# Seven-product down projection in five up steps instead of seven or eight, its weights loaded earlier, and four half products moved behind the last up product

## The reference

```python
def conv_ffn(x, w_up, conv_k, conv_b, w_down):        # first block, D_FF = 2816
    h = x @ w_up                                      # 1024 -> 2 * 2816
    ...
    h = sum(hp[:, j:j + S] * conv_k[j] for j in range(CONV_W)) + conv_b
    a, b = jnp.split(h, 2, axis=-1)
    return (jax.nn.gelu(a, approximate=False) * b) @ w_down

def swiglu(xn, w_gate, w_up, w_down):                 # second block, D_FF_2 = 2816
    return (jax.nn.silu(xn @ w_gate) * (xn @ w_up)) @ w_down
```

## Time and profile before

| what | value |
|---|---|
| median of 3 runs | 3492.47 us (3491.96 to 3493.58) |
| profiled execution: its time, its span | 3492.06 us, 3490.3 us |
| TensorE busy | 3372.2 us, 97% of the span, 16655 matmuls and transposes |
| VectorE, ScalarE busy | 2205.2 us (63%), 1475.6 us (42%) |
| mean granted TensorE clock | 0.991 of full speed |
| mean HBM traffic | 90 GB/s |

### The profile page before, as it was taken

The page is one execution under the profiler, slowest core; times in us unless marked ns, Lnnn a source line. Parts: engine busy times, 40 slices in busy tenths (PEclk is TensorE's granted clock), DMA queues, the critical chain, the costliest instruction groups (busy, mean ns, idle before and its releaser), DMA issues. The chain is left out here.

```text
span 3490.3 us, 42076 instructions
## 1 busy us (share of the span) xinstructions
PE 3372.2 (97%) x16655; PEld 2815.0 (81%) x16655; DVE 2205.2 (63%) x3566; ACT 1475.6 (42%) x2577; POOL 252.3 (7%) x319
## 2 busy tenths in 40 slices
PE   9999999999999999999999999999999999999999
PEld 7888888877788888888777777888888887888887
DVE  5644566777766545677777686554666697545665
ACT  4543333433335433334333564544343574543332
POOL 1300210000023002000000020100000000100000
PEclk9999999999999999999999999999999999999999
DMA  4112342232131122413221222423222212413321
GB/s 159 58 52 72 104 159 66 103 103 97 61 122 61 52 79 95 162 61 109 97 97 61 84 70 79 130 63 119 86 85 102 96 43 66 130 55 106 105 103 61
DMA packets 84148, 315.14 MB, mean 90 GB/s; under 512 B 10096, under 2 KB 10864, under 8 KB 78832
## 3 DMA queue, kind: packets, MB, share of 16 engines
q1 hardware_dynamic: 83952, 312.46, 27.2%
HBM read 308.23 MB, written 4.19 MB: 90 GB/s over the span
## 5 line engine op out<-in xcount | busy, mean ns | idle before, releaser
L1344 PE MATMUL bk<-xh,wh 128*128 128x512 f32 (+1 forms) x2216 | 838.3, 378 | 5.7 <-DVE xl L2070 5.6
L1344 PE MATMUL bk<-xh,wl 128*128 128x512 f32 (+1 forms) x2216 | 830.3, 375 | 0.0
L1344 PE MATMUL bk<-xl,wh 128*128 128x512 f32 (+1 forms) x2216 | 830.0, 375 | 0.0
L2057 DVE TENSOR_TENSOR wl<-wr,wh 128x1024 fp32r<-128x1024 f32 (+1 forms) x300 | 361.9, 1215 | 302.4 <-ACT wh L1650 301.1
L1344 PEld LDWEIGHTS bk<-xh,wh 128*128 128x128 f32 x2216 | 418.0, 189 | 79.8 <-issue 4.1
L1344 PEld LDWEIGHTS bk<-xh,wl 128*128 128x128 f32 x2216 | 417.6, 188 | 75.6
L1344 PEld LDWEIGHTS bk<-xl,wh 128*128 128x128 f32 x2216 | 418.0, 189 | 72.1
L1650 ACT ACTIVATE wh<-wr 128x1024 fp32r<-128x1024 f32 (+1 forms) x300 | 310.2, 1043 | 313.8 <-PE bk L1344 218.7
L2063 DVE SCALAR_TENSOR_TENSOR wl<-wr,par,wh 128x512 fp32r<-128x512 f32 (+1 forms) x360 | 249.3, 737 | 166.5 <-ACT wh L1656 165.3
L1623 ACT ACTIVATE wh<-ar 128x1024 fp32r<-128x1024 f32 (+1 forms) x168 | 141.1, 843 | 487.0 <-DVE ar L2028 271.0
L1656 ACT ACTIVATE wh<-wr,par 128x512 fp32r<-128x512 f32 (+1 forms) x360 | 236.1, 708 | 202.4 <-PE bk L1344 153.4
(11 more groups left out here) (292 smaller groups left out, 5368.1 us busy)
## 6 DMA issues: line engine op xcount, KB each, us to landing
wr<-in_wpk SPq DMA_DIRECT2D x468, 512.0 KB, 3.6
ar<-in_wdn SPq DMA_DIRECT2D x36, 1024.0 KB, 7.8
gb<-in_ln_g SPq DMA_DIRECT2D x6, 512.0 KB, 4.5
gb<-in_ln_b SPq DMA_DIRECT2D x6, 512.0 KB, 6.3
ar<-in_xT SPq DMA_DIRECT2D x8, 256.0 KB, 7.3
wr<-in_wpk SPq DMA_DIRECT2D x8, 256.0 KB, 6.2
ar<-in_memT SPq DMA_DIRECT2D x2, 1024.0 KB, 4.7
x<-in_x SPq DMA_DIRECT2D x4, 512.0 KB, 5.2
```

The lines of the kernel that those rows point to most:

```text
L1344: i = pe.e.matmul(dst, lw, rw, start=g not in opened, stop=end)
L2057: dve.e.tensor_tensor(m.wl[:, s, a], m.wr[:, r, a], m.wh[:, s, a].bitcast(F32), ALU.subtract) \
```

## The change

Three things are changed in every one of the four FFNs.

1. In phases 0 and 1 the fourteen half products followed the up steps in numbers 0, 2, 2, 2 (first pair) and 2, 2, 2, 2 (second pair), none in the third pair. Now they follow in 0, 3, 3, 3 and 3, 2, 0, 0: five up steps of the eight. The next phase's three raw down transfers stood in up steps 1, 2 and 3 of the third pair; now they stand in up steps 2 and 3 of the second pair and 0 of the third.
2. In phase 2 the numbers were 0, 3, 3, 2 for pair 9 and 3, 3, 0, 0 for pair 10. Now they are 0, 3, 3, 2 and 2, 0, 0, 0, and the last four half products (7a, 7b, 4a, 4b) stand behind pair 10's last up step.
3. So that pairs 9 and 10 can be split before products 7 and 4 have read the old hidden values, their split values go to places that these two products don't read: three quarters where the sums were, one quarter behind the buffer. `hid_hi` and `hid_lo` of these pairs become two instructions each (768 and 256 columns), and wait for product 3 instead of 4. Pair 9's are put in up steps 1 and 2 of pair 10, pair 10's behind 7a and 7b.

```diff
-        def made(pair, seven=None, per=(0, 0, 0, 0), after=0, loads=None):
+        def made(pair, seven=None, per=(0, 0, 0, 0), loads={}):
             for step, _ in enumerate(ups(2 * pair)):
-                if loads is not None and step in (1, 2, 3):
-                    self.add("down_load", *loads, 3 * loads[0].ph + step - 1, l)
+                if step in loads:
+                    self.add("down_load", *loads[step], l)
                 if seven is None:
                     if self.soon:
                         self.add(*self.soon.pop(0))
-                elif step < 2 and pair % 3 == 0 and self.soon:
+                elif self.soon and (pair % 3 == 0 and step < 2 or pair == 10 and step > 0):
                     self.add(*self.soon.pop(0))
...
         made(0)
-        made(1, loads=(F[0], None))
+        made(1, loads={n + 1: (F[0], None, n) for n in range(3)})
         made(2)
-        for ph in range(3):
-            products = self.seven(F[ph])
-            pair = 3 * ph + 3
-            made(pair, products, (0, 2, 2, 2) if ph < 2 else (0, 3, 3, 2))
-            if ph < 2:
-                made(pair + 1, products, (2, 2, 2, 2))
-                drive((products, 1))
-                made(pair + 2, loads=(F[ph + 1], F[ph]))
-            else:
-                held, self.soon = self.soon, []
-                steps = ups(2 * pair + 2)
-                for step in range(4):
-                    next(steps)
-                    if step < 2:
-                        for _ in range(3):
-                            next(products, None)
-                    if step == 1:
-                        drive((products, 1))
-                        self.soon = held
-                    elif self.soon:
-                        self.add(*self.soon.pop(0))
-                drive((steps, 1))
-                self.soon += [("hid_hi", si, 10), ("hid_lo", si, 10)]
+        for ph in range(2):
+            products, pair = self.seven(F[ph]), 3 * ph + 3
+            made(pair, products, (0, 3, 3, 3))
+            made(pair + 1, products, (3, 2, 0, 0), {n + 2: (F[ph + 1], F[ph], pair + n) for n in range(2)})
+            made(pair + 2, loads={0: (F[ph + 1], F[ph], pair + 2)})
+        products = self.seven(F[2])
+        made(9, products, (0, 3, 3, 2))
+        made(10, products, (2, 0, 0, 0))
+        for _ in products:
+            if self.soon:
+                self.add(*self.soon.pop(0))
...
     def hid(self, side, pair, b, n):
-        a = pair % 3 * 1792 + b * 256
+        a = pair % 3 * 1792 + b * 256 if b < 7 else 5376 + (pair - 9) * 256
...
     def hid_hi(si, pair):
         if pair >= 3:
-            act.wait_ge(*ev["grp7", si, pair // 3 - 1, 4, 1])
+            act.wait_ge(*ev["grp7", si, pair // 3 - 1, 4 if pair < 9 else 3, 1])
```

More of the change, by code:

```diff
@@ L1316, in mm @@
                         pe.wait_ge(*ev["hid", G.si, kb // 2])
-                        xh, xl = (m.hid(side, kb // 2, 2 * (kb % 2), 512).unsqueeze(1) for side in (m.hh, m.hl))
-                        kb = 0
+                        b, at = 2 * (kb % 2) + o // 2, o % 2 * 128
+                        xh, xl = (m.hid(side, kb // 2, 4 + b, 256)[:, at:at + 128] for side in (m.hh, m.hl))
                     elif G.op == "branch" and G.base == 8:
@@ L1338, in mm @@
                 else:
-                    seq = [(xh[:, kb, tile(o)], wh[:, kk, :]), (xh[:, kb, tile(o)], wl[:, kk, :]),
-                           (xl[:, kb, tile(o)], wh[:, kk, :])]
+                    if G.op != "hid":
+                        xh, xl = xh[:, kb, tile(o)], xl[:, kb, tile(o)]
+                    seq = [(xh, wh[:, kk, :]), (xh, wl[:, kk, :]), (xl, wh[:, kk, :])]
                     dst = ps[:, 0:cols]
@@ L1631, in hid_hi @@
                 act.wait_ge(*ev["prod", si, 2 * pair + p])
-            act.e.activation(m.hid(m.hh, pair, 0, 1024), m.z(si, pair), ACT.Copy) \
+            z = m.z(si, pair)
+            act.e.activation(m.hid(m.hh, pair, 4, 768), z[:, 0:768], ACT.Copy)
+            act.e.activation(m.hid(m.hh, pair, 7, 256), z[:, 768:1024], ACT.Copy) \
                 .then_inc(*ev.up("x_hi", ("hid_hi", si, pair)))
@@ L2011, in hid_lo @@
         dve.wait_ge(*ev["hid_hi", si, pair])
-        i = dve.e.tensor_tensor(m.hid(m.hl, pair, 0, 1024), m.z(si, pair), m.hid(m.hh, pair, 0, 1024).bitcast(F32),
+        if pair >= 9:
+            z = m.z(si, pair)
+            dve.e.tensor_tensor(m.hid(m.hl, pair, 4, 768), z[:, 0:768], m.hid(m.hh, pair, 4, 768).bitcast(F32),
                                 ALU.subtract)
-        if pair >= 9:
-            i.then_inc(*ev.up("x_lo", ("hid", si, pair)))
+            dve.e.tensor_tensor(m.hid(m.hl, pair, 7, 256), z[:, 768:1024], m.hid(m.hh, pair, 7, 256).bitcast(F32),
+                                ALU.subtract).then_inc(*ev.up("x_lo", ("hid", si, pair)))
             return
+        dve.e.tensor_tensor(m.hid(m.hl, pair, 0, 1024), m.z(si, pair), m.hid(m.hh, pair, 0, 1024).bitcast(F32),
+                            ALU.subtract)
         dve.e.tensor_tensor(m.hid(m.hl, pair, 4, 768), m.zx[pair % 2], m.hid(m.hh, pair, 4, 768).bitcast(F32),
```

## The result

The changed kernel takes 3460.59 us (median of 4 runs, 3458.5 to 3461.48) against 3492.58 us before: a ratio of 0.9907, interval 0.989 to 0.9924. It is 32.0 us faster. I had forecast 3451 with a range of 3441 to 3466; the likeliest case's own range, 3446 to 3457, does not hold it. The profiled execution took 3458.5 us, 33.6 less than the profiled one of before and 2.1 less than the median of its own kernel.

The account below looks back on a forecast made before the run. TensorE, busy for 97% of the span, was taken as the bound, so only its gaps and half-clock time could pay. -36.0 + 16.2 - 21.2 = -41.0 us gave 3451 us, range 3441 to 3466 (8 in 10).

Parts of the forecast that it names:

- the likeliest case: The prediction's own case, all three parts as summed: 3451 us, own range 3446 to 3457, chance 0.67.
- The late starts: Phases 1 and 2 of the first two FFNs: earlier down transfers make four starts prompt, giving back 36.0 us.
- The gaps between 2b and 5a: Phases 0 and 1: 5a waits for product 2's additions, adding 2.02 us in each of eight phases, +16.2 us.
- the rival's 13 us: Rival at the eight new gaps: half clock follows each, 1.67 us apiece, 13.4 us in all, 3464.5 us; chance 0.10.
- A wrong bound in that step: Lower bound of each new gap between 2b and 5a: one addition (0.73 us) and the refill, about 1 us.
- The FFN end: End of all four FFNs: waits for the split of pairs 9 and 10 and excess time go, -21.2 us.
- The chain I built: First FFN's end: ScalarE and VectorE work up to pair 10's weight split, done E + 13.4, due 13.6 us.
- E: The end time of the last up step at the FFN end, from which the prediction counts pair 10's preparation.
- the rivals: Five outcomes: clock falls (0.10), pair 10's split late (0.08), shorter gaps (0.07), starts still late (0.05), transfers starve up steps (0.03).

Follow-up runs that it names:

- e1: The kernel before with only the three down transfers moved to where the change has them: 3460.07 us, ratio 0.9909.
- e3: The changed kernel with the three down transfers back in up steps 1, 2 and 3 of the third pair: 3484.61 us, ratio 0.9977.
- e11: The changed kernel with product 4's two additions moved behind the first token tile's residual additions and norm: 3459.48 us, ratio 0.9903.
- e6: The changed kernel with product 2's two additions put ahead of the weight split on VectorE: 3440.36 us, ratio 0.9847.
- e4: The kernel before with only the FFN end changed (last four half products, places of pairs 9 and 10): 3473.82 us, ratio 0.9947.
- e7: The changed kernel with half products of phases 0 and 1 at 0, 4, 2, 3 and 3, 2, 0, 0: 3440.46 us, ratio 0.9847.

## Why the prediction was right, and where its sizes were off

- **The late starts.** Right in mechanism and nearly in size. The transfer held the evacuation: e1 gave 32.4 us, the sum said 36.0, and 2.8 of the difference are the gaps that grew in phase 2. The wait that I had worked out as 0.2 us is 0.16 us in the trace, but a wait costs more than its length: from one matmul start to the next, each start keeps 0.42 us, 0.9 us more in all.
- **The gaps between 2b and 5a.** Right in place and number (eight new ones), too small in size: 16.2 forecast, 19.8 us in the trace. The unit of 2.02 us was taken, for the first two FFNs, from phases that had just started late, and a late start gave VectorE time to catch up. With prompt starts the gap is 2.51 us in phases 1 and 2 of the first two FFNs, the old phase 2 included (e1 shows the same lengthening, with its spread untouched), and with late ones it is 2.02 again (e3, with the dense spread). In phase 1 ScalarE's high split ahead of the gap now waits for VectorE's differences, where in phase 0 it waited for TensorE:

```profile
769.57 1.06 ACT L1612 ACTIVATE wh<-ar 128x1024 fp32r<-128x1024 f32 x1 [2.58 <-DVE ar L2023]
```

  Four gaps that are 0.49 us longer and one with half clock behind it, 1.6 us, make the 3.6 us. The Trainium skill's page "TensorE: Matmul & The Clock Gate", section "A second HAM failure mode: psum-queue depth-cycling", tells of a clock that goes back and forth because TensorE idles briefly and often between groups. The trace agrees with it in one gap of twelve here, e11's in three of twelve, and the rival's 13 us, a fall at each of eight, did not come. That there was only one in the profiled execution is partly luck.
- **A wrong bound in that step.** "An addition starts only when 2b ends", and so at least 1 us would remain: e6 leaves 0.47. Each bank has an addition of its own, and the first bank is full half a half product earlier. My 1 us left that out.
- **The FFN end.** Right: 21.2 us forecast, and no gap is left. (e4, with this end alone, gained 18.7 us. That is the 21.2 less the 2.7 of the next point, to 0.2 us.) The chain I built ended with the weight split at E + 13.4. In the trace E is 910.56, the multiplications end at E + 4.1, pair 10's low split near E + 11.6, and TensorE reaches it at E + 13.6:

```profile
913.41 1.29 DVE L2303 TENSOR_TENSOR ar<-ar 128x512 f32<-128x512 f32 x2
...
918.08 2.92 DVE L2040 TENSOR_TENSOR x<-x,bk 128x512 f32<-128x512 f32 x4
...
921.78 0.42 DVE L2007 TENSOR_TENSOR al<-ar,ah 128x256 fp32r<-128x256 f32 x1
```

- **What was left out.** The stretch behind the FFN end: +1.26 and +1.40 us in the first two FFNs. I had followed VectorE's chain only as far as TensorE needs pair 10, and put what lies behind at nothing. Which part of the new end does it is open (e11).
- **The account.** 0.9 + 3.6 + 2.7 = 7.2 us of the 7.4 by which the profiled execution (-33.6) missed the sum (-41.0). The remaining 2.1 us of the distance to the median lie between one execution and its median; in e1 to e11 the runs of one kernel lie 1 to 6 us apart, and the number of falls of the clock can be a part of that, as e11's profile shows. Every term that was off was off to the slower side, so nothing cancelled: the 3460.6 us stand inside the range of 3441 to 3466, which I had made wide for the rivals, and outside that of my own case.

## What to carry to other kernels

When work is packed more densely, ask who now stands beside whom: here 31.6 us hung on whether an up step stands between a product and the one that takes over its PSUM banks, and nothing on the density itself once the transfers came early. An evacuation that frees a bank should stand ahead of work that merely looks ahead on the same engine. And a gap's size must be taken from a place with the same history: a wait upstream hides part of the next one, and removing the first makes the second longer.

## What I had not expected of the hardware

A gap of the same kind and length is followed by half clock at one place and not at another, and in one execution and not in the next. In the changed kernel it was one of twelve waits of 1.7 to 2.3 us, with a granted clock of 0.82 over that window and 1.00 over the two others shown; in e11 it was three of the same twelve. Sorted by length, the waits of 5a for product 2's additions look less like chance. In the eight traces that have such waits (before, the change, e1 to e4, e7, e11), none of 42 waits of 1.74 us had half clock behind it, and eight of fourteen waits of 2.2 to 2.6 us had. Each of the eight cost about 1.6 us. That the length alone decides is not shown: the longer waits are all in phases 1 and 2 of the first two FFNs.
